# The inverse multiplied into b and r_b once for all chunks, in the RWKV part of a two-layer decoder trunk

## The chip, the cores and the metric

One core of one Trainium2 chip runs the whole program. The metric is the device time of that core in microseconds (us). A hardware profile of one execution gives the span and what each engine did when: TensorE (PE, with its weight loads PEld), VectorE (DVE), ScalarE (ACT), GpSimd (POOL) and SyncE (SP), which issues most transfers.

## The reference

Two decoder layers over 256 tokens of width 1024. Each layer projects x, runs a sparse multi-query attention and an RWKV-7 time mix side by side, gates and adds their outputs, projects, normalizes, and ends with a convolutional GLU. The change is inside the time mix, whose core is a recurrence over tokens, for 16 heads of 64:

```python
def step(state, inp):
    r_t, w_t, k_t, v_t, kk_t, b_t = inp
    sa = jnp.einsum('bhvk,bhk->bhv', state, -kk_t)
    state = state * w_t[:, :, None, :] + sa[..., None] * b_t[:, :, None, :] + v_t[..., None] * k_t[:, :, None, :]
    return state, jnp.einsum('bhvk,bhk->bhv', state, r_t)
```

The kernel computes it in chunks of 64 tokens: within a chunk the sequential dependence is a triangular system, whose inverse is built once per chunk, and the state is carried from chunk to chunk.

## The kernel before

**Rounds and units.** A round is 4 heads (GROUPS = 4 rounds a layer, 8 in all; r = 4*layer + g). It has GB = 2 blocks of 128 partitions (two heads each, 64 partitions a head) and NCH = 4 chunks, so NU = 8 units of 128 x 64. `wkv` (L976) writes out what TensorE does in a round, with semaphores between it and the other engines; ScalarE's and VectorE's parts are in their own loops (L1635 and L2342).

**A round.** Gram matmuls (L992) need, from the round before, `y_sum` on VectorE and `rkV` on ScalarE. Then LEVELS = 6 levels build the inverse: TensorE computes W = nT*X and XW = Y*W, ScalarE copies W out, VectorE updates X under a mask and transposes it into Y. The last level (L1062) computes `WtY` by `joined`, two 32 x 32 matmuls a unit, and VectorE updates Y with it; X isn't completed. Then come the steps over the chunks c = 0 to 3 (L1095 to L1130): 

- Z: the carried state S is multiplied with a and r (`Z{c}`, not for c = 0); VectorE adds akV (`chunk_z`, L1920).
- Q: Y times Z, together with rk times V for this chunk; ScalarE copies Q from PSUM to `Qs` (`chunk`, L1491).
- S and y: bt times Qs gives the state's update, rb times Qs the chunk's output; VectorE makes the new state (`chunk_s`, L1930).

At the end VectorE adds the outputs (`y_sum`, L1943), then centers them.

**Dense pieces.** TensorE's waits in a round are filled with pieces of the projections x*W (rkv of the next round, gates, and so on). A piece is 2 of 8 blocks of a product for one weight slot: six 128x256 matmuls, since each float32 product is made of three rounded ones (`product`, L768: hi*hi, hi*lo, lo*hi). Four pieces use up one weight slot. A round has 32 pieces and so eight slots. The tables LEVEL_GAPS and CHUNK_GAPS say in which gap each piece goes; `fill(n)` issues those of gap n. The chunk steps hold 20 pieces (19 in the last round of a layer), in gaps 14 to 24.

**Mids.** Before TensorE can use a slot, ScalarE casts it into `mid_hi` (L1342) and VectorE subtracts that from the slot (L1758). There are two `mid_hi` buffers, so the cast for slot m waits until TensorE has used slot m-2. `mids_up_to(mids_by(gap))`, at fixed places in both engines' code, makes those whose buffer is free by that gap; the places decide what stands behind what in these queues. Refills of the weight ring (four slots) are issued by SP as slots are used.

**Preparation of the next round** (not in the last round of a layer) is mixed into the steps: on TensorE `prep_1`, `prep_v`, `prep_rnT`, `prep_rnx` (L869); on ScalarE two tanh (L1413) and `prep_exp` (L1416: three exponentials and one more map); on VectorE decay and scan, `prep_keys`, `prep_keys_scaled`, `prep_arc`, `prep_bk`, and `prep_v` (three operations, layer 1 only).

**Helpers seen in the rows.** L930 is `per_head`, L936 `crossed`, L961 `swapped`: each issues one matmul per head, 64 x 64, for a unit. A float32 matmul of that kind has two records. In a chunk block a `per_head` and a `swapped` or `crossed` go side by side.

Of the kernel before, what the change touches and what calls it, by code (L numbers as in the profile page):

```python
# [66 lines left out]
CH = 64  # L67
# [18 lines left out]
CHUNK_GAPS = ([[14, 14, 14, 15, 17, 17, 18, 18, 19, 19, 20, 20, 21, 21, 22, 22, 23, 23, 24, 24]] * (GROUPS - 1)  # L86
              + [[14, 14, 15, 16, 16, 17, 17, 18, 19, 19, 20, 20, 21, 22, 22, 23, 23, 24, 24]])
# [3 lines left out]
GAPS = 14 + 3 * NCH  # L91
# [121 lines left out]
def trunk(nc, x_in, pos_in, stream, lora_in, cpar_in, rpar_in, const_in, masks_in, out, x_dram, v_dram):  # L213
    ctx = ExitStack()
    with ctx:
# [292 lines left out]
        def norm_steps(l, w):  # L508
            if l == DEPTH - 1 and w == "B":
# [42 lines left out]
                                    [f"XW{l}{k}" if l < LEVELS - 1 else f"WtY{l}{k}" for k in range(2)]) for l in lv], [])  # L552
                          + sum([[f"Z{c}"] * (c > 0) + [f"Q{c}"] + ([f"S{c}"] if c < NCH - 1 else []) + [f"y{c}"]
                                 for c in range(NCH)], []))
# [6 lines left out]
                           + [f"Q{c}" for c in range(NCH - 1)] + ["rkV_first", f"Q{NCH - 1}", "rkV"])  # L561
        act_y = by_round("act_y", ["sq", "yn"])
        dve_wkv = by_round("dve_wkv", ["Y0", "X0", "nTrb", "akrk"]
                           + sum([([f"X{l}{k}"] if l < LEVELS - 1 else []) + [f"Y{l}{k}"] for l in lv for k in range(2)], [])
# [153 lines left out]
        def _(pe):  # L718
# [257 lines left out]
            def wkv(r, fill):  # L976
# [58 lines left out]
                for lev in range(2, LEVELS):  # L1035
                    for k in range(2):
# [4 lines left out]
                        for u in range(4 * k, 4 * k + 4):  # L1041
                            dst = half64("W", k)[:, u - 4 * k, :]
                            if lev < BLOCKED:
                                w = per_head(dst, nT, X[:, u, :], u)
                            elif lev < LEVELS - 1:
                                w = per_block(dst, nT, X, u)
                            else:
                                w = across(dst, nT, X, u, 0, block_cols(1), block_cols(0))
                            if u == 4 * k + 3:
                                w.then_inc(*pe_wkv.inc(r, f"W{lev}{k}"))  # L1050
                            if lev == LEVELS - 1 and k == 1:
                                wty = joined(u - 4)
                            if lev == 2 and u < len(step_units):
                                if u == 0:
                                    pe.wait_ge(*act_wkv(r, "tokK"))
                                v = step_units[u]
                                side = swapped(unit64(5)[:, u, :], kt[:, v, :], Vc[:, v, :])
                                if u == len(step_units) - 1:
                                    side.then_inc(*pe_wkv.inc(r, "ktV"))
                        if k == 0:  # L1060
                            fill(2 + 2 * lev)
                    if lev == LEVELS - 1:  # L1062
                        wty.then_inc(*pe_wkv.inc(r, f"WtY{lev}0"))
# [3 lines left out]
                        for u in range(4, NU):  # L1067
                            wty = joined(u)
                        wty.then_inc(*pe_wkv.inc(r, f"WtY{lev}1"))
# [23 lines left out]

                pe.wait_ge(*act_wkv(r, "ktV"))
                for c in range(NCH):  # L1095
                    if c:
                        pe.wait_ge(*dve_wkv(r, f"S{c - 1}"))
                    s_old = S[:, (c + 1) % 2, :, :]
                    y = [unit64(5)[:, u, :] for u in bc(c)]
                    if c:  # L1100
                        for b, u in enumerate(bc(c)):
# [4 lines left out]
                    fill(14 + 3 * c, c == 0)  # L1106
                    pe.wait_ge(*dve_wkv(r, f"Z{c}" if c else f"Y{LEVELS - 1}1"))
                    if c == 0 and g + 1 < GROUPS:
                        pe.wait_ge(*act_prep(r + 1, "thw"))
                    if c == NCH - 1:  # L1110
                        pe.wait_ge(*act_wkv(r, "rkV_first"))
# [8 lines left out]
                    pe.wait_ge(*act_wkv(r, f"Q{c}"))  # L1120
                    for b, u in enumerate(bc(c)):
                        if c < NCH - 1:
                            mm = per_head(step64(2)[:, b, :], bt, Qs[:, b, :], u)
                            if b == GB - 1:
                                mm.then_inc(*pe_wkv.inc(r, f"S{c}"))
                        mm = crossed(y[b], rb, Qs[:, b, :], u, start=(c == 0), stop=(c == 0 or b == GB - 1))
# [3 lines left out]
                    fill(16 + 3 * c)  # L1130
# [194 lines left out]
        def _(act):  # L1325
# [165 lines left out]
            def chunk(r, c):  # L1491
                act.wait_ge(*pe_wkv(r, f"Q{c}"))
                act.copy(Qs[:, :, :], step64(3)).then_inc(*act_wkv.inc(r, f"Q{c}"))

            def rkv_out(r, c):

                steps = {NCH - 2: range(NCH - 1), NCH - 1: [NCH - 1]}.get(c, [])
                if len(steps):
                    n, a = len(steps), steps[0] * GB * CH
                    src = ps[:, 7, a:a + n * GB * CH].rearrange("p (c b s) -> p c b s", b=GB, s=CH)  # L1500
                    dst = yt[:, :, :].rearrange("p (b c) s -> p c b s", b=GB)[:, steps[0]:steps[0] + n]
                    for q, o in zip(HEADS, OTHER):
                        last = act.copy(dst[o], src[q])
                    last.then_inc(*act_wkv.inc(r, "rkV" if c == NCH - 1 else "rkV_first"))

            for l in L2:
# [128 lines left out]
                for g in range(GROUPS):  # L1635
# [41 lines left out]
                    for c in range(NCH):  # L1677
                        mids_up_to(l, mids_by(GAPS * g + 13 + 3 * c))
# [64 lines left out]
        def _(dve):  # L1743
# [158 lines left out]
            def level(r, lev):  # L1902
                for k in range(2):
                    if lev < LEVELS - 1:
                        dve.wait_ge(*pe_wkv(r, f"XW{lev}{k}"))
                        update(r, X, f"X{lev}{k}", 1, lev, k)
# [8 lines left out]
                    else:  # L1915
                        dve.wait_ge(*pe_wkv(r, f"WtY{lev}{k}"))
                        update(r, Y, f"Y{lev}{k}", 0, lev, k)
# [237 lines left out]
            for l in L2:  # L2155
# [186 lines left out]
                for g in range(GROUPS):  # L2342
# [25 lines left out]
                    for c in range(NCH):  # L2368
                        if c:
# [3 lines left out]
                            mids_up_to(l, mids_by(GAPS * g + 13 + 3 * c))  # L2373
# [20 lines left out]
                        if c in (1, 2):  # L2394
                            mids_up_to(l, mids_by(GAPS * g + 15 + 3 * c))
# [161 lines left out]
```

## Time and profile before

| | us |
|---|---|
| median of 3 runs | 1107.33 (1106.68 to 1109.58) |
| the profiled execution | 1107.22 |
| its span | 1105.4 |
| PE busy | 1077.7 (97%) |
| DVE busy | 802.7 (73%) |
| ACT busy | 569.6 (52%) |

Times in the rows below are us from the start of the span. A row of a timeline has start, duration, engine, line, operation, output and inputs, shapes and count; what stands in brackets is the engine's idle time before it and what ended that. Matmuls overlap one another, so from one matmul to the next the starts count, not the durations.

### The profile page before, as it was taken

To read this page: it belongs to the slowest core of one execution; us is meant where nothing else is said; L and a number is where in the kernel's file an instruction comes from. 1 tells how busy PE (TensorE), PEld (TensorE's weight loads), DVE (VectorE), ACT (ScalarE), POOL (GpSimd) and SP (SyncE) were. 2 spreads that over 40 slices of the span, in tenths; PEclk is the share of its full clock that TensorE was granted. 3 is DMA by queue.
4 is the path that set the end of the run, shared out by engine and by line. 5 is a ranking of instruction groups with operands and counts; after the bars stand their busy time and mean duration, and the time that the engine had idled before them with its cause. 6 is when DMAs were issued, how large, how long until landed. Compare 5 with 4: busy or idle time off the path is not lost. (4 is left out here: it accounts for less than half of the span.)

```text
span 1105.4 us, 31915 instructions
## 1 busy us (share of the span) xinstructions
PE 1077.7 (97%) x13568; PEld 977.2 (88%) x13568; DVE 802.7 (73%) x1471; ACT 569.6 (52%) x1008; POOL 72.2 (7%) x61
## 2 busy tenths in 40 slices
PE   8999999999999999999999999999999999999996
PEld 8878888888997999998898888888888979999885
DVE  3678787868676877774557887878876778777645
ACT  3653555555544555553246445555565445555531
POOL 0000010101001000000100000202011010000001
PEclk9999999999999999999999999999999999999998
DMA  8533232322564666566474323222326637566661
GB/s 302 166 102 118 72 101 80 95 90 89 191 229 135 211 190 189 186 200 197 134 236 142 121 88 98 89 86 81 98 64 229 210 128 226 189 185 189 210 188 56
DMA packets 45526, 165.58 MB, mean 150 GB/s; under 512 B 5168, under 2 KB 5424, under 8 KB 45136
## 3 DMA queue, kind: packets, MB, share of 16 engines
q1 hardware_dynamic: 42736, 154.03, 43.4%
q0 software_dynamic: 1504, 7.47, 2.2%
q8 instruction: 108, 1.77, 0.7%
q10 hardware_dynamic: 1152, 2.10, 0.6%
q14 instruction: 26, 0.21, 0.1%
HBM read 160.44 MB, written 3.15 MB: 148 GB/s over the span
## 5 line engine op out<-in xcount | busy, mean ns | idle before, releaser
L771 PE MATMUL ps<-x_tok_r,mid_hi 128*128 128x256 f32 x576 | 177.1, 307 | 0.5 <-DVE ring_r L1758 0.5
L773 PE MATMUL ps<-x_tok_r,ring_r 128*128 128x256 f32 x576 | 162.2, 282 | 0.0
L772 PE MATMUL ps<-yb_hi,mid_hi 128*128 128x256 f32 x576 | 162.1, 281 | 0.0
L1758 DVE TENSOR_TENSOR ring_r<-ring,mid_hi 128x1024 fp32r<-128x1024 f32 x80 | 97.2, 1216 | 31.1 <-ACT mid_hi L1342 31.0
L771 PEld LDWEIGHTS ps<-x_tok_r,mid_hi 128*128 128x128 f32 x576 | 108.5, 188 | 9.5 <-issue 1.4
L772 PEld LDWEIGHTS ps<-yb_hi,mid_hi 128*128 128x128 f32 x576 | 108.9, 189 | 0.7 <-issue 0.7
L773 PEld LDWEIGHTS ps<-x_tok_r,ring_r 128*128 128x128 f32 x576 | 108.9, 189 | 0.0
L1342 ACT CAST mid_hi<-ring 128x1024 fp32r<-128x1024 f32 x80 | 83.8, 1048 | 34.3 <-PE ps L773 26.6
L2021 DVE TENSOR_TENSOR rs_ks_r<-ring,tha_kkn_r 128x1024 fp32r<-128x1024 f32 x44 | 53.9, 1224 | 19.9 <-ACT tha_kkn_r L1394 19.7
L2021 DVE TENSOR_TENSOR vs_dC_r<-ring,b_k_r 128x1024 fp32r<-128x1024 f32 x44 | 53.7, 1220 | 17.6 <-ACT b_k_r L1394 17.6
L2021 DVE TENSOR_TENSOR X_Y_r<-ring,arc_r 128x1024 fp32r<-128x1024 f32 x42 | 51.3, 1222 | 19.8 <-ACT arc_r L1394 19.8
L2021 DVE TENSOR_TENSOR w_lo<-ring,w_hi 128x1024 fp32r<-128x1024 f32 x42 | 51.4, 1224 | 18.0 <-ACT w_hi L1394 17.9
L1394 ACT CAST tha_kkn_r<-ring 128x1024 fp32r<-128x1024 f32 x44 | 45.9, 1044 | 32.9 <-PE ps L773 32.9
L1394 ACT CAST arc_r<-ring 128x1024 fp32r<-128x1024 f32 x42 | 43.8, 1043 | 28.8 <-PE ps L773 19.6
L1394 ACT CAST b_k_r<-ring 128x1024 fp32r<-128x1024 f32 x44 | 45.9, 1043 | 20.1 <-PE ps L773 20.1
L772 PE MATMUL ps<-oT_r,tha_kkn_r 128*128 128x256 f32 x192 | 54.0, 281 | 0.0
L772 PE MATMUL ps<-oT_r,b_k_r 128*128 128x256 f32 x192 | 53.6, 279 | 0.0
L772 PE MATMUL ps<-oT_r,arc_r 128*128 128x256 f32 x192 | 53.6, 279 | 0.0
L772 PE MATMUL ps<-oT_r,w_hi 128*128 128x256 f32 x192 | 53.5, 279 | 0.0
L1394 ACT CAST w_hi<-ring 128x1024 fp32r<-128x1024 f32 x42 | 43.8, 1044 | 15.5 <-PE ps L773 15.2
L771 PE MATMUL ps<-xT_r,tha_kkn_r 128*128 128x256 f32 x176 | 49.9, 283 | 0.6 <-DVE oT_r L2103 0.6
L773 PE MATMUL ps<-xT_r,rs_ks_r 128*128 128x256 f32 x176 | 49.4, 281 | 0.0
(487 smaller groups left out, 3326.0 us busy)
## 6 DMA issues: line engine op xcount, KB each, us to landing
ring<-stream_dram SPq DMA_DIRECT2D x281, 512.0 KB, 3.7
lora_w<-lora_dram POOLq DMA_DIRECT2D x2, 1536.0 KB, 7.2
W_bt<-rpar_dram POOLq DMA_DIRECT2D x4, 512.0 KB, 5.1
kt_V<-rpar_dram POOLq DMA_DIRECT2D x4, 512.0 KB, 7.1
x_tok<-x_dram SPq DMA_DIRECT2D x2, 512.0 KB, 4.7
v_saved_dram<-vs_dC ACTq DMA_DIRECT2D x4, 256.0 KB, 4.5
x_tok<-x_dram SPq DMA_DIRECT2D x1, 1024.0 KB, 6.2
vf<-v_saved_dram ACTq DMA_DIRECT2D x4, 256.0 KB, 3.8
```

The costliest lines, as they stand in the source:

```text
L771: pe.matmul(dst, lh, rh, start=start, stop=False)
L772: pe.matmul(dst, lh, rl, start=False, stop=False)
L773: return pe.matmul(dst, ll, rh, start=False, stop=stop)
L1342: act.copy(mid_hi[m % NM][:, :], ring[:, n % RING, :]).then_inc(*act_mid.inc(l, m))
L1394: act.copy(w_hi[m % NS], ring[:, n % RING, :]).then_inc(*act_split.inc(l, m))
L1758: dve.tensor_tensor(rounded["ring"][:, k, :], ring[:, k, :], f32(mid_hi[m % NM][:, :]), ALU.subtract).then_inc(*dve_mid.inc(l, m))
L2021: dve.tensor_tensor(w_lo[m % NS], ring[:, n % RING, :], f32(w_hi[m % NS]), ALU.subtract).then_inc(*dve_split.inc(l, m))
```

## The change

Q is gone. Since Q = Y*Z is only used as bt*Q and rb*Q, the inverse is multiplied into bt and rb instead, for all chunks at once and ahead of the steps (`byX` on TensorE, `by_x` on ScalarE). A step then has two blocks, Z and S with y, and uses Z (or akV) where it used Qs. For this X is what must be complete, so the last level updates the left half of X instead of the right half of Y. All rk*V products move into the `byX` block, and ScalarE copies them out at once in step 1. GAPS is 23 instead of 26, the same pieces lie in gaps 14 to 21, and the calls of `mids_up_to` and `pairs_done` get new gap numbers; some of them are no longer limited to steps 1 and 2.

```diff
-CHUNK_GAPS = ([[14, 14, 14, 15, 17, 17, 18, 18, 19, 19, 20, 20, 21, 21, 22, 22, 23, 23, 24, 24]] * (GROUPS - 1)
-              + [[14, 14, 15, 16, 16, 17, 17, 18, 19, 19, 20, 20, 21, 22, 22, 23, 23, 24, 24]])
+CHUNK_GAPS = ([[14, 14, 14, 15, 15, 16, 16, 17, 17, 18, 18, 18, 19, 19, 19, 20, 20, 20, 21, 21]] * (GROUPS - 1)
+              + [[14, 14, 15, 15, 16, 16, 16, 17, 17, 18, 18, 18, 19, 19, 19, 20, 20, 21, 21]])
-GAPS = 14 + 3 * NCH
+GAPS = 15 + 2 * NCH
-    return [p for p, n in ends if n >= 14 and (n - 14) // 3 == c]
+    return [p for p, n in ends if n >= 14 and max(n - 15, 0) // 2 == c]
...
             def joined(u):
 
-                return across(half64("XW", u // 4)[:, u % 4, :], W, Y, u, 1, block_cols(0), block_cols(1))
+                for h in range(2):
+                    q = block_rows(h, 1)
+                    mm = pe.matmul(half64("XW", u // 4)[q, u % 4, 0:HB], Y[q, u, block_cols(1)], W[q, u, block_cols(0)],
+                                   start=True, stop=True)
+                return mm
...
+                fill(14, 1)
+                pe.wait_ge(*dve_wkv(r, f"X{LEVELS - 1}1"))
                 pe.wait_ge(*act_wkv(r, "ktV"))
+                if g + 1 < GROUPS:
+                    pe.wait_ge(*act_prep(r + 1, "thw"))
+                early = sum([bc(c) for c in range(NCH // 2)], [])
+                late = sum([bc(c) for c in range(NCH // 2, NCH)], [])
+                for i in range(len(early) + NU):
+                    if i < len(step_units):
+                        u = step_units[i]
+                        per_head(unit64(3)[:, u, :], X, bt[:, u, :], u)
+                    elif i < len(step_units) + len(late):
+                        u = late[i - len(step_units)]
+                        per_head(unit64(5)[:, u, :], X, rb[:, u, :], u)
+                    if i < len(early):
+                        u = early[i]
+                        mm = crossed(unit64(2)[:, u, :], X, rb[:, u, :], u)
+                    else:
+                        u = i - len(early)
+                        mm = swapped(rkv64(u % NCH)[:, u // NCH, :], rk[:, u, :], Vc[:, u, :])
+                mm.then_inc(*pe_wkv.inc(r, "byX"))
                 for c in range(NCH):
...
-                    fill(14 + 3 * c, c == 0)
-                    pe.wait_ge(*dve_wkv(r, f"Z{c}" if c else f"Y{LEVELS - 1}1"))
...
-                    for b, u in enumerate(bc(c)):
-                        swapped(rkv64(c)[:, b, :], rk[:, u, :], Vc[:, u, :])
-                        mm = per_head(step64(3)[:, b, :], Y, Zs[:, b, :] if c else akV[:, u, :], u)
-                    mm.then_inc(*pe_wkv.inc(r, f"Q{c}"))
-                    fill(15 + 3 * c)
+                    fill(15 + 2 * c)
...
-                    pe.wait_ge(*act_wkv(r, f"Q{c}"))
+                    pe.wait_ge(*(dve_wkv(r, f"Z{c}") if c else act_wkv(r, "rbX")))
                     for b, u in enumerate(bc(c)):
+                        z = Zs[:, b, :] if c else akV[:, u, :]
                         if c < NCH - 1:
-                            mm = per_head(step64(2)[:, b, :], bt, Qs[:, b, :], u)
+                            mm = per_head(step64(2)[:, b, :], bt, z, u)
...
-                    fill(16 + 3 * c)
+                    fill(16 + 2 * c)
...
+            def by_x(r):
+
+                act.wait_ge(*pe_wkv(r, "byX"))
+                dst, src = [t.rearrange("p (b c) s -> p b c s", b=GB)[:, :, 0:NCH - 1] for t in (bt, unit64(3))]
+                act.copy(dst, src).then_inc(*act_wkv.inc(r, "btX"))
+                dst, crossed, own = [t.rearrange("p (b c) s -> p b c s", b=GB) for t in (rb, unit64(2), unit64(5))]
+                for q, o in zip(HEADS, OTHER):
+                    act.copy(dst[q, :, 0:NCH // 2], crossed[o, :, 0:NCH // 2])
+                act.copy(dst[:, :, NCH // 2:], own[:, :, NCH // 2:]).then_inc(*act_wkv.inc(r, "rbX"))
...
                     for c in range(NCH):
-                        mids_up_to(l, mids_by(GAPS * g + 13 + 3 * c))
+                        mids_up_to(l, mids_by(GAPS * g + (14 + 2 * c if c else 13)))
...
-                        chunk(r, c)
+                        if c == 0:
+                            by_x(r)
                         if c == 0 and nxt:
                             prep_exp(r + 1)
-                        if c in (1, 2):
-                            mids_up_to(l, mids_by(GAPS * g + 15 + 3 * c))
-                        rkv_out(r, c)
+                        mids_up_to(l, mids_by(GAPS * g + 15 + 2 * c))
+                        if c == 1:
+                            rkv_out(r)
...
                 if lev == LEVELS - 1:
-                    out, mask, src = out[:, :, HB:CH], mask[:, :, HB:CH], src[:, :, 0:HB]
+                    out, mask, src = out[:, :, 0:HB], mask[:, :, 0:HB], src[:, :, 0:HB]
...
-                            mids_up_to(l, mids_by(GAPS * g + 13 + 3 * c))
+                            mids_up_to(l, mids_by(GAPS * g + 14 + 2 * c))
...
-                        if c in (1, 2):
-                            mids_up_to(l, mids_by(GAPS * g + 15 + 3 * c))
+                        mids_up_to(l, mids_by(GAPS * g + 15 + 2 * c))
                         if nxt and c == 0:
                             prep_pend(r + 1)
```

## Rows read from the trace of the kernel before

**Rows 1.** The page: span, and busy time of the engines

```profile
span 1105.4 us, 31915 instructions
...
PE 1077.7 (97%) x13568; PEld 977.2 (88%) x13568; DVE 802.7 (73%) x1471; ACT 569.6 (52%) x1008; POOL 72.2 (7%) x61
```

**Rows 2.** Who waited for whom, TensorE: total, times, longest

```profile
PE ps L869 <- DVE ang L1803: 0.7, 3, 0.2
```

**Rows 3.** Stretches: length, then busy time (and instructions) of each engine

```profile
668.38:693.48 25.10, 24.84 (x330) 21.96 (x324) 19.33 (x39) 14.91 (x32) 1.64 (x1) 1.00 0.30 92
...
173.14:198.02 24.88, 24.54 (x326) 21.69 (x322) 17.91 (x38) 14.41 (x30) 1.65 (x1) 1.00 0.31 90
```

**Rows 4.** Timeline of TensorE, 670 to 675 us, a round of layer 1

```profile
670.19 0.39 PE L771 MATMUL ps<-x_tok_r,mid_hi 128*128 128x256 f32 x1
...
671.81 0.27 PE L961 MATMUL ps<-kt_V,ak_rk 64*64 64x64 f32 x2
...
671.82 0.27 PE L930 MATMUL ps<-sq,X_Y 64*64 64x64 f32 x2
...
671.91 0.23 PE L961 MATMUL ps<-kt_V,ak_rk 64*64 64x64 f32 x2
...
672.04 0.23 PE L930 MATMUL ps<-sq,X_Y 64*64 64x64 f32 x2
...
672.20 0.39 PE L771 MATMUL ps<-x_tok_r,mid_hi 128*128 128x256 f32 x1
...
673.46 0.27 PE L930 MATMUL ps<-Qs,W_bt 64*64 64x64 f32 x2
...
673.90 1.15 PE L869 MATMUL ps<-ang,const 8*128 8x128 f32 x8
...
674.98 0.27 PE L930 MATMUL ps<-S,arc 64*64 64x64 f32 x2
```

**Rows 5.** The same, step 2, and the end of the round

```profile
683.22 0.27 PE L961 MATMUL ps<-kt_V,ak_rk 64*64 64x64 f32 x2
...
691.87 0.28 PE L772 MATMUL ps<-yb_hi,mid_hi 128*128 128x256 f32 x1
...
693.05 0.28 PE L773 MATMUL ps<-x_tok_r,ring_r 128*128 128x256 f32 x1
...
693.48 0.33 PE L930 MATMUL ps<-arc,b_k 64*64 64x128 f32 x2
```

**Rows 6.** Timeline of ScalarE in the same round

```profile
672.34 0.27 ACT L1493 COPY Qs<-ps 128x128 f32<-128x128 f32 x1 [0.47 <-PE ps L930]
...
673.68 0.63 ACT L1420 ACTIVATE dA<-dB 128x512 f32<-128x512 f32 x1 [1.08 <-DVE vs_dC L1790]
...
676.25 1.03 ACT L1342 CAST mid_hi<-ring 128x1024 fp32r<-128x1024 f32 x1
...
684.99 0.96 ACT L1503 COPY yt<-ps 64x384 f32<-64x384 f32 x2
```

**Rows 7.** Timeline of VectorE in the same round

```profile
677.31 1.23 DVE L1758 TENSOR_TENSOR ring_r<-ring,mid_hi 128x1024 fp32r<-128x1024 f32 x1 [1.34 <-ACT mid_hi L1342]
...
678.45 0.87 DVE L1749 SCALAR_TENSOR_TENSOR rs_ks<-ps,cpar,rs_ks 128x255 f32<-128x255 f32 x2
...
680.01 0.29 DVE L1938 TENSOR_TENSOR Sa<-ps,Sa 128x128 f32<-128x128 f32 x1
...
680.54 0.68 DVE L1840 TENSOR_TENSOR rs_ks<-rs_ks,tmp 128x512 f32<-128x512 f32 x1
...
682.88 0.28 DVE L1923 TENSOR_TENSOR Zs<-ps,sq 128x128 f32<-128x128 f32 x1
...
685.80 0.29 DVE L1938 TENSOR_TENSOR Sa<-ps,Sa 128x128 f32<-128x128 f32 x1
...
690.59 0.69 DVE L1814 TENSOR_TENSOR scratch<-vf,vs_dC 128x512 f32<-128x512 f32 x1
...
692.65 0.68 DVE L1947 TENSOR_TENSOR yt<-ps,yt 128x512 f32<-128x512 f32 x1
```

More of the change, by code:

```diff
@@ L551, in trunk @@
                                  + (["XW10", "XW11", "akV"] if l == 1 else
-                                    [f"XW{l}{k}" if l < LEVELS - 1 else f"WtY{l}{k}" for k in range(2)]) for l in lv], [])
-                          + sum([[f"Z{c}"] * (c > 0) + [f"Q{c}"] + ([f"S{c}"] if c < NCH - 1 else []) + [f"y{c}"]
-                                 for c in range(NCH)], []))
+                                    [f"XW{l}{k}" for k in range(2)]) for l in lv], [])
+                          + ["byX"] + sum([[f"Z{c}"] * (c > 0) + [f"S{c}"] * (c < NCH - 1) + [f"y{c}"] for c in range(NCH)], []))
         pe_bonus = Steps(sem("pe_bonus"), [["zg", "bonus"] if r % GROUPS else ["bonus", "zg"] for r in range(R)])
@@ L560, in trunk @@
                                                                            for l in lv], [])
-                           + [f"Q{c}" for c in range(NCH - 1)] + ["rkV_first", f"Q{NCH - 1}", "rkV"])
+                           + ["btX", "rbX", "rkV"])
         act_y = by_round("act_y", ["sq", "yn"])
         dve_wkv = by_round("dve_wkv", ["Y0", "X0", "nTrb", "akrk"]
-                           + sum([([f"X{l}{k}"] if l < LEVELS - 1 else []) + [f"Y{l}{k}"] for l in lv for k in range(2)], [])
+                           + sum([[f"X{l}{k}"] + [f"Y{l}{k}"] * (l < LEVELS - 1) for l in lv for k in range(2)], [])
                            + sum([[f"Z{c}", f"T{c}"][0:2 if c < NCH - 1 else 1] * (c > 0) + [f"S{c}a", f"S{c}"] * (c < NCH - 1)
@@ L1067, in wkv @@
                         for u in range(4, NU):
-                            wty = joined(u)
-                        wty.then_inc(*pe_wkv.inc(r, f"WtY{lev}1"))
+                            xw = joined(u)
+                        xw.then_inc(*pe_wkv.inc(r, f"XW{lev}1"))
                         continue
@@ L1119, in wkv @@
                         prep_rnT(r + 1)
-                    pe.wait_ge(*act_wkv(r, f"Q{c}"))
+                    pe.wait_ge(*(dve_wkv(r, f"Z{c}") if c else act_wkv(r, "rbX")))
                     for b, u in enumerate(bc(c)):
+                        z = Zs[:, b, :] if c else akV[:, u, :]
                         if c < NCH - 1:
-                            mm = per_head(step64(2)[:, b, :], bt, Qs[:, b, :], u)
+                            mm = per_head(step64(2)[:, b, :], bt, z, u)
                             if b == GB - 1:
                                 mm.then_inc(*pe_wkv.inc(r, f"S{c}"))
-                        mm = crossed(y[b], rb, Qs[:, b, :], u, start=(c == 0), stop=(c == 0 or b == GB - 1))
+                        mm = crossed(y[b], rb, z, u, start=(c == 0), stop=(c == 0 or b == GB - 1))
                     mm.then_inc(*pe_wkv.inc(r, f"y{c}"))
@@ L1489, in levels, with rkv_out @@
                     act.copy(ktV[:, :, :], unit64(5)[:, 0:(NCH - 1) * GB, :]).then_inc(*act_wkv.inc(r, "ktV"))
[L1491 to L1504, printed above, removed]
+            def by_x(r):
[6 more added lines that the diff above has]
+                act.copy(dst[:, :, NCH // 2:], own[:, :, NCH // 2:]).then_inc(*act_wkv.inc(r, "rbX"))
+            def rkv_out(r):
+                src = ps[:, 7, :].rearrange("p (c b s) -> p c b s", b=GB, s=CH)
+                dst = yt[:, :, :].rearrange("p (b c) s -> p c b s", b=GB)
+                for q, o in zip(HEADS, OTHER):
+                    last = act.copy(dst[o], src[q])
+                last.then_inc(*act_wkv.inc(r, "rkV"))
             for l in L2:
@@ L1903, in level @@
                 for k in range(2):
+                    dve.wait_ge(*pe_wkv(r, f"XW{lev}{k}"))
+                    update(r, X, f"X{lev}{k}", 1, lev, k)
                     if lev < LEVELS - 1:
[L1905 to L1906 removed]
                         dve.wait_ge(*dve_wkv(r, f"X{lev}{k}"))
```

16 lines of the change are left out of this document (4 added, 12 removed).

## The prediction

> **What bounds the kernel now.** The page first: TensorE shows work for 1077.7 of 1105.4 us [rows 1]. The list of who waited for whom then says how little of TensorE's time around this change is waiting: of the waits that touch these steps the largest listed one is 0.7 us in three pieces [rows 2]. So the kernel is bound by what TensorE has to issue, and a change can win only by giving it less, and loses as soon as it makes it wait. The busy time by stretches gives the size of the stage: from the first dense piece of gap 14 to the first Gram matmul of the next round it is 25.10 us in a round of layer 1 and 24.88 us in one of layer 0, with VectorE busy for 19.33 and 17.91 of it [rows 3]. In layer 1 VectorE has under 6 us of slack in the stage, and takes its work strictly in the order of the code.
>
> Then the timelines of one such round, engine by engine. On TensorE a chunk step is a block of four 64-row slots: it begins 1.62 us after the first matmul of two dense pieces, and the next dense matmul begins 0.39 later; one block with its two pieces takes 2.01 us [rows 4]. A dense piece alone costs 6 matmuls at 0.118 (691.87 to 693.05, ten from start to start) [rows 5], 0.70 us: so the block costs 2.01 - 1.41 = 0.60, of which the slots are 4 x 0.06 (671.91 to 672.04, two slots) and the rest, 0.36, is going into the small form and back out.
>
> **TensorE's own work.** Before, the four Q blocks of a round cost 4 x 0.60 = 2.40 us (the rk*Vc matmuls ride in the same slots). They become one block of 12 iterations, each of two slots: 0.60 + 20 x 0.06 = 1.80. That is 0.60 us less in each of 8 rounds, 4.8 in all, although there are 12 more products. The last level still has two matmuls per unit, with other rows and columns; the old and the new pair differ in the column block that they share with the W matmuls. No row has that pairing in 32-row form, so I bound it by nothing and by one slot of 0.06 for each of 8 units, 0.5 us a round; I take nothing, because in 64-row form L961 and L930 share column halves and start 0.01 apart [rows 4].
>
> At that same place the Trainium skill, "TensorEngine Tiling (Array Packing)", section "Restrictions and Gotchas", says that different row tiles can't access one PSUM bank at the same time. Taken for both heads of a product, that would double the 24 slots, 1.44 us a round. The row with L961 x2 and L930 x2 (each pair is two heads, one bank) shows them starting together, so the trace speaks against it here.
>
> Waits that the new order removes, if nothing else goes wrong: Q of step 2 starts at 683.22 where the rhythm (674.98 + 4 x 2.01) gives 683.02, 0.2 late, right behind Zs on VectorE [rows 4, 5, 7]; there are six such rounds, 1.2 us. The matmuls of L869 (eight rows) wait 0.7 us in three rounds [rows 2]. The Gram matmuls of layer 1 start 0.43 after the last dense matmul instead of 0.21, three times 0.2 [rows 5]. Together 2.5 at most.
>
> **The new order, walked through** in a round of layer 1 with the rows' durations. byX starts at 671.81 as Q0 did, its last slot at 671.81 + 0.10 + 22 x 0.06 = 673.23, and the next dense matmul at 673.39. ScalarE begins 0.30 after a last slot [rows 4, 6]. Its copies into b and r_b have 384 columns and three times 256. The nearest row is 64x384 twice in 0.96 [rows 6]; from that and the 0.27 for 128 columns I take 0.42 + 3 x 0.32 = 1.4 us (at least four of the 0.27, 1.1; at most four of 0.48, 1.9). They end at 674.93. TensorE meanwhile does two pieces and the two small prep products, and wants r_b at 675.35: this wait costs nothing. It would cost once the copies take more than 1.8.
>
> But behind them on ScalarE stand prep_exp, 673.68 to 676.25, 2.57 us, which used to run beside Q0 and step 0, and then the cast of the fifth dense slot (rows say 1.03) [rows 6]. They end at 677.50 and 678.53. On VectorE the subtraction of that slot now stands ahead of pend and Z1 (before: behind Z1), so VectorE waits for ScalarE until 678.56 and is done at 679.79. TensorE by then: step 0 at 675.35, L869 at 675.79, dense at 676.87 (it took 1.08), Z1 at 678.49, dense at 678.89, and the fifth slot's first piece at 679.70. It waits 0.15.
>
> VectorE then has, without a gap: pend, Z1 and T 0.5 (three of its smallest operations, 0.1 to 0.2 each), the shift-add and the keys 1.56, the S pair 0.53, the scaled keys and the sixth slot 2.34 + 0.09 [rows 7]: ready at 684.8. TensorE has in the same time the rest of gap 17, step 1, the three pieces of gap 18 and Z2, and wants the sixth slot, now the first piece of gap 19 (it was in gap 21), at 683.77. **First real stall: 1.1 us.** Next, step 2 of VectorE gets the third shift-add in front of arc and b, k: Z2, T, arc, b and k 2.92, a slot 1.14, the shift-add 0.78, the S pair 0.53: counted from 684.7, where Z2 begins, S2 is ready at 690.1, and TensorE asks at 689.89: 0.2 us.
>
> The end of the round is worse. A new call at the end of step 3 puts the subtraction for the next round's second slot ahead of y_sum. VectorE: Z3 690.73, a slot to 692.08, v (layer 1 only, 690.59 to 692.65, 2.06) to 694.14, the new slot 1.14 to 695.28, y_sum 0.68 to 695.96. The Gram matmuls wait for y_sum. TensorE arrives at 694.24, since only two pieces and not four stand between Z3 and y3. **Stall 1.8 us**, Gram at 696.0 where it was at 693.48 [rows 5]: +2.5 a round. In layer 0 v is absent, but the new slot's cast can start only when TensorE has used the last slot (about 692.1), so cast 1.05, subtraction 1.23 and y_sum 0.65 end at 695.0; the round is 26.6 long against 24.88, +1.75 [rows 3].
>
> The last round of each layer has no prep: VectorE has gaps there, and the saved 0.60 stays. And since y_sum is now the releaser, the centering and the masks that follow it come later relative to the Gram matmuls: y_sum began 0.83 ahead of them [rows 5, 7], now 0.72; in layer 0, without v, it must have been further ahead, for which I have no row. Between 0.1 and 0.5, I put 0.2 on each of six rounds. The shift of a subtraction out of the next round saves TensorE nothing, as that one stood behind the masks and had no reader waiting. Loads on SP's queue keep their order and count; POOL is not touched.
>
> Sum: 3 x 2.5 + 3 x 1.75 - 2 x 0.6 + 6 x 0.2 = +12.75 us. The profiled execution took 1107.22 us, 0.11 under the median of the three runs, so the sum goes on it unchanged: **1120.0 us**.
>
> **Rivals.** (1) Faster: TensorE's own work decides. 4.8 + 2.5 less is 1099.9 us. For it: TensorE is busy throughout, and the saving in blocks is plain. It needs VectorE to have the sixth slot by 683.77, one microsecond earlier than walked, and y_sum by 694.2; that is so only if copies and prep_exp together hold ScalarE under about 2.9 us where I count 4.0. Against it: prep_exp alone is 2.57. Chance 0.15.
> (2) Only the end of the round waits: the middle stalls dissolve as VectorE catches up, and 1.0 us (layer 0) to 1.3 (layer 1) are left: -7.3 + 3 x 1.0 + 3 x 1.3 = -0.4, 1106.8 us. For it: VectorE has 1.34 us idle ahead of the fifth slot in the old trace [rows 7]. Against it: that very idle time is what the later cast takes. Chance 0.12.
> (3) More than forecast: the 32-row matmuls at their upper bound, 8 x 0.5, and the copies at 1.9, which moves the whole chain behind them, 6 x 0.5: 7 more, 1127 us. Chance 0.07.
> (4) The two heads of a product exclude each other in a bank and byX takes 48 slots: 8 x 1.44 = 11.5 more, less what the stalls hide, some 1125 us. Against it: the pairs that start together [rows 4]. Chance 0.01. The Trainium skill has this rule, in "TensorEngine Tiling (Array Packing)", "Restrictions and Gotchas".
>
> The forecast has 0.65.
>
> **Numbers.** 0.3% (3.3 us) is about what a measurement of this kernel can tell from no change. Faster has rival 1 and a little of 2, 0.16; the same has most of 2, 0.11; slower 0.73. The forecast's own range is 1114 to 1125 us, from stalls 1 us smaller in each of six rounds to copies and late masks at their upper bounds. The range given takes in rival 2 and rival 3, 1104 to 1127; rival 1 lies outside.
>
> **What would show it.** Right: byX as one run of about 1.45 us; six waits of TensorE for the sixth slot's subtraction (L1758's successor) of about 1 us; Gram matmuls released by y_sum, 1 us late in layer 0 and near 2 in layer 1; the stage at 26.6 us in layer 0 and 27.6 in layer 1; the last rounds shorter by 0.6. Wrong: the same stretches at or under 24.9 with VectorE's subtraction ahead of TensorE, or a wait of TensorE for r_b, which I hold at nothing.

## The result, and the profile after

The changed kernel takes 1121.28 us (median of 6 runs, 1119.04 to 1123.88) against 1107.01 us for the kernel before on the same chip: ratio 1.0128, interval 1.0105 to 1.0152, 1.3% slower. The profiled execution took 1122.55 us with a span of 1120.7 us, 15.3 more than before.

The head of the page, kernel after:

```profile
span 1120.7 us, 32270 instructions
...
PE 1079.5 (96%) x13760; PEld 981.3 (88%) x13760; DVE 801.7 (72%) x1471; ACT 573.5 (51%) x992; POOL 72.4 (6%) x61
```

TensorE's busy time is 1.8 us longer than in [rows 1], so of the 15.3 us almost all (13.5) is TensorE standing still. For whom, the list of waits says (kernel after, TensorE: total, times, longest):

```profile
PE ps L929 <- DVE yt L1961: 8.8, 6, 1.8
PE ps L770 <- DVE ring_r L1775: 6.8, 10, 0.9
```

The first line was not there before, and of the second kind there was one wait of 0.5 us. L929 is the Gram matmul of the next round, which waits for y_sum; L770 is a dense piece that waits for its subtraction. Both are VectorE's.

The busy time by stretches, kernel after: a stage of layer 1, one of layer 0, and the one of layer 0's last round (up to the first matmul of o_hi with tha_kkn_r); columns as in [rows 3]:

```profile
677.00:704.56 27.56, 24.74 (x353) 22.09 (x348) 20.18 (x40) 15.89 (x30) 1.64 (x1) 1.00 0.31 100
121.45:148.39 26.94, 24.50 (x351) 21.84 (x346) 18.28 (x37) 15.16 (x28) 1.64 (x1) 1.00 0.29 94
285.36:304.85 19.49, 19.36 (x311) 17.69 (x307) 11.97 (x21) 10.75 (x16) 0.00 (x0) 1.00 0.49 164
```

Against [rows 3] that is +2.46 us in layer 1 and +2.06 in layer 0, and the three rounds of each layer agree within 0.01. The last rounds went from 19.89 to 19.49, -0.40. Over all eight stages (3 x 2.46 + 3 x 2.07 - 0.78): +12.8 of the 15.3 us. The levels between the stages add 1.35, the rest of the kernel 1.1.

TensorE's timeline, kernel after, round of layer 1: the byX block with the dense matmuls around it, the sixth slot, the Gram.

```profile
680.21 0.28 PE L772 MATMUL ps<-x_tok_r,ring_r 128*128 128x256 f32 x1
680.42 0.27 PE L929 MATMUL ps<-W_bt,X_Y 64*64 64x64 f32 x2
680.43 0.27 PE L935 MATMUL ps<-nT_rb,X_Y 64*64 64x64 f32 x2
680.53 0.23 PE L929 MATMUL ps<-W_bt,X_Y 64*64 64x64 f32 x2
...
681.98 0.39 PE L770 MATMUL ps<-x_tok_r,mid_hi 128*128 128x256 f32 x1
...
693.54 0.36 PE L770 MATMUL ps<-x_tok_r,mid_hi 128*128 128x256 f32 x1 [0.92 <-DVE ring_r L1775]
...
704.56 0.33 PE L929 MATMUL ps<-arc,b_k 64*64 64x128 f32 x2 [1.77 <-DVE yt L1961]
```

byX takes 1.56 us from its first matmul to the next dense one. The last line answers to 693.48 in [rows 5]: then the Gram waited 0.2 us at most, starting 0.43 after the last dense matmul where the pitch is 0.21.

ScalarE, kernel after, same round: the three kinds of by_x copies, prep_exp's first line, and the cast of the fifth slot.

```profile
682.10 0.48 ACT L1508 COPY W_bt<-ps 128x384 f32<-128x384 f32 x1 [1.62 <-PE ps L964]
682.61 0.75 ACT L1511 COPY nT_rb<-ps 64x256 f32<-64x256 f32 x2
683.37 0.38 ACT L1512 COPY nT_rb<-ps 128x256 f32<-128x256 f32 x1
683.63 0.63 ACT L1433 ACTIVATE dA<-dB 128x512 f32<-128x512 f32 x1
...
686.19 1.04 ACT L1355 CAST mid_hi<-ring 128x1024 fp32r<-128x1024 f32 x1
```

VectorE, kernel after, same round: the subtractions for slots five and six, and the end of the stage:

```profile
687.26 1.23 DVE L1775 TENSOR_TENSOR ring_r<-ring,mid_hi 128x1024 fp32r<-128x1024 f32 x1 [2.13 <-ACT mid_hi L1355]
...
692.18 1.22 DVE L1775 TENSOR_TENSOR ring_r<-ring,mid_hi 128x1024 fp32r<-128x1024 f32 x1
...
701.99 0.69 DVE L1837 SCALAR_TENSOR_TENSOR vs_dC<-scratch,vs_dC 128x512 f32<-128x512 f32 x1
702.59 1.22 DVE L1775 TENSOR_TENSOR ring_r<-ring,mid_hi 128x1024 fp32r<-128x1024 f32 x1
703.73 0.68 DVE L1961 TENSOR_TENSOR yt<-ps,yt 128x512 f32<-128x512 f32 x1
```

Read it from below: y_sum ends at 704.41 and the Gram starts 0.15 later; ahead of y_sum stands a subtraction that no one needs before the next round's levels. From 687.26 on VectorE is idle once for 0.55 us (ahead of Z3). The one large gap is the 2.13 us in front of the fifth slot, for ScalarE's cast behind prep_exp.

Layer 0 ends otherwise. ScalarE and VectorE there, kernel after, ahead of the Gram at 148.39:

```profile
145.34 1.05 ACT L1355 CAST mid_hi<-ring 128x1024 fp32r<-128x1024 f32 x1 [2.52 <-PE ps L772]
...
146.42 1.23 DVE L1775 TENSOR_TENSOR ring_r<-ring,mid_hi 128x1024 fp32r<-128x1024 f32 x1 [1.34 <-ACT mid_hi L1355]
147.56 0.68 DVE L1961 TENSOR_TENSOR yt<-ps,yt 128x512 f32<-128x512 f32 x1
```

VectorE has no v here and is idle for 1.34 us: it waits for the cast, and the cast for TensorE's last matmul on the buffer. So in layer 1 the stage ends by VectorE's own queue, in layer 0 by the hand-over from TensorE to ScalarE to VectorE.

### The profile page after: what moved, and what is told of

It is laid out like the page before. It is cut to its first block, busy times and chain, and to the rows that moved or that the text cites. A ratio compares the mean times of both kernels' runs of the same rounds, so it can differ in the third digit from the quotient of the medians.

```text
span 1120.7 us, 32270 instructions
## 1 busy us (share of the span) xinstructions
PE 1079.5 (96%) x13760; PEld 981.3 (88%) x13760; DVE 801.7 (72%) x1471; ACT 573.5 (51%) x992; POOL 72.4 (6%) x61
## 4 chain that ended last, share of the span: by engine, by line
PE 78%; DVE 14%; ACT 4%; issue 3%; DMA 1%; POOL 1%; DVEq 0%; SPq 0%; ACTq 0%
PE ps L770 19%; PE ps L771 18%; PE ps L772 17%; PE ps L929 5%; PE ps L1156 3%; DVE ring_r L1775 3%; PE ps L745 2%; PE ps L943 2%; PE ps L970 1%; PE ps L1214 1%; PE ps L1230 1%; ACT mid_hi L1355 1%; PE ps L964 1%; DMA ring<-stream_dram 1%; PE ps L884 1%
## 5 line engine op out<-in xcount | busy, mean ns | idle before, releaser
L770 PE MATMUL ps<-x_tok_r,mid_hi 128*128 128x256 f32 x576 | 176.4, 306 | 7.1 <-DVE ring_r L1775 6.8
L770 PEld LDWEIGHTS ps<-x_tok_r,mid_hi 128*128 128x128 f32 x576 | 108.6, 189 | 17.1 <-issue 7.5
L1900 DVE COPY_PREDICATED X_Y<-masks,ps 128x256 f32<-128x256 uint32 (+1 forms) x80 | 33.0, 415 | 29.8 <-PE ps L929 17.8
L770 PE MATMUL ps<-xT_r,tha_kkn_r 128*128 128x256 f32 x176 | 49.4, 281 | 0.6 <-DVE oT_r L2117 0.6
```

The costliest lines, as they stand in the source:

```text
L770: pe.matmul(dst, lh, rh, start=start, stop=False)
L1900: dve.copy_predicated(out, mask, src).then_inc(*dve_wkv.inc(r, name))
```

## The experiments

The theory: the stage is now set by one serial chain, ScalarE's cast of the fifth slot, then VectorE's queue up to S of step 2, and from there to y_sum by one of the two ends above, so that work on that chain costs up to its own length. The rival: TensorE's work, or the products over all chunks, is the cost itself. All but e8 start from the changed kernel. Stage lengths are read like those above, for one round of each kind; the other rounds of the kind agree within 0.03 us, but for one round each of e2, e4, e6, e10 and e11, which is 0.06 to 0.17 longer (in e10 and e11 a stretch at half the clock reaches into it). The ratio is to the kernel before as run beside each experiment (medians 1106.32 to 1107.01 us), so it is the better of the two to compare. There is no e9.

| run | time, us | ratio to before | stage, layer 0 | layer 1 | last round |
|---|---|---|---|---|---|
| before | 1107.01 | 1 | 24.87 | 25.10 | 19.89 |
| after | 1121.28 | 1.0128 (1.0105 to 1.0152) | 26.94 | 27.56 | 19.49 |
| e1 | 1117.46 | 1.0096 (1.0078 to 1.0114) | 25.70 | 26.41 | 19.48 |
| e2 | 1116.85 | 1.0097 (1.0076 to 1.0119) | 26.08 | 26.91 | 19.49 |
| e3 | 1119.48 | 1.0131 (1.0099 to 1.0163) | 26.92 | 27.55 | 19.48 |
| e4 | 1112.56 | 1.0052 (1.0037 to 1.0067) | 24.88 | 25.80 | 19.48 |
| e5 | 1110.21 | 1.0031 (1.0008 to 1.0053) | 24.87 | 25.79 | 19.48 |
| e6 | 1105.07 | 0.9982 (0.9966 to 0.9998) | 24.07 | 25.27 | 19.49 |
| e7 | 1109.43 | 1.0027 (1.0016 to 1.0039) | 24.09 | 24.30 | 19.49 |
| e8 | 1116.96 | 1.0080 (1.0057 to 1.0103) | 26.11 | 26.23 | 19.88 |
| e10 | 1104.80 | 0.9976 (0.9962 to 0.9990) | 24.09 | 24.28 | 19.48 |
| e11 | 1123.45 (one run) | | 27.43 | 28.05 | 19.98 |

**e1: y_sum ahead of the last subtraction** (VectorE alone)

```
                        if nxt and c == 1:
                            prep_keys_scaled(r + 1)
-                       mids_up_to(l, mids_by(GAPS * g + 15 + 2 * c))
+                       if c < NCH - 1 or not nxt:
+                           mids_up_to(l, mids_by(GAPS * g + 15 + 2 * c))
...
                    y_sum(r)
                    if nxt:
+                       mids_up_to(l, mids_by(GAPS * g + 15 + 2 * (NCH - 1)))
                        prep_bonus(r + 1)
```

> The changed kernel, and on VectorE alone the last subtraction of step 3 (the one that belongs to the next round's second gap) is issued behind y_sum instead of ahead of it, in the six rounds that have a next round. Theory (that subtraction waits for its cast and so delays y_sum, for which the gram waits): TensorE's idle time before the gram falls from 1.15 us to under 0.3 in layer 0 and from 1.8 to under 0.8 in layer 1, three times each; the time falls by 4 to 7 us, to 1114 to 1117 us. Rival (the added time is TensorE's own work, the last-level products over all chunks are no cheaper in the end): the idle time before the gram may fall, but what follows it starts no earlier, and the time stays within 1 us of 1121.

TensorE's waits in e1:

```profile
PE ps L929 <- DVE yt L1961: 1.9, 3, 0.6
PE ps L970 <- DVE ak_rk L1886: 3.6, 6, 0.8
```

The Gram's wait fell from 8.8 to 1.9 us and the stage by 1.24 and 1.15 us. In layer 1 that is about the subtraction (1.23) gone from VectorE's queue. In layer 0 the likeness to 1.23 is chance: there cast and subtraction together left the path, and what TensorE got back is the 1.21 us that it had waited in front of the Gram. But the subtraction now stands ahead of the masked products, and half of the gain comes back as a wait for ak_rk in the first level. The time fell by 3.8 us, just short of the 4 to 7 expected.

**e2: the fifth cast ahead of prep_exp** (ScalarE alone)

```
                        if c == 0 and nxt:
+                           mids_up_to(l, mids_by(GAPS * g + 15))
                            prep_exp(r + 1)
```

> The changed kernel, and ScalarE casts the fifth slot's piece between the copies of byX and the exponentials of the next round, instead of behind them. Theory (the fifth subtraction stands ahead of pend and Z1 on VectorE and idles there 2.1 us): that subtraction starts about 2.6 us earlier, the idle time before the sixth slot's dense piece (0.9 us) falls to 0.3 or less unless the exponentials, now 1 us later, delay the keys; time 1 to 5 us under 1121. Rival (the exponentials set the pace: pend and the keys wait for them): the subtraction is earlier but pend and all behind it are 1 us later, gram later; time 1121 to 1127.

The stages fell by 0.86 and 0.65 us, the time by 4.4: inside the 1 to 5 expected, near the upper end. The fifth subtraction came 2.2 us earlier, where 2.6 was expected; only a part of that is gained, since VectorE then waits 1.24 us for Z1. TensorE's longest wait for a subtraction fell from 0.9 to 0.6 us and not to 0.3.

**e3: the sixth subtraction ahead of the scaled keys** (VectorE alone)

```
                        if nxt and c == 1:
+                           mids_up_to(l, mids_by(GAPS * g + 15 + 2 * c))
                            prep_keys_scaled(r + 1)
```

> The changed kernel, and VectorE does the subtraction for the sixth slot ahead of the scaled keys instead of behind them. Theory (the sixth slot's dense product waits for a subtraction that is queued behind 1.2 us of work it does not need): the 0.9 us of idle time before it go, six times; but y_sum at the end waits for casts as before, so that part of it comes back at S2 or the gram: time 1116 to 1121. Rival (TensorE's order is set by something else): no change, within 1 us of 1121.

```profile
PE ps L929 <- DVE yt L1961: 8.8, 6, 1.8
PE ps L929 <- DVE S L1954: 6.0, 6, 1.0
```

The waits of e3 show what a stall in the middle was worth: nothing. The sixth slot's wait went, a new one of 1.0 us for S came in each of six rounds, and the stages are the same within 0.02 us. Exchanging two operations on the chain leaves its end where it was, as the theory says for the Gram. The whole time says less: the median is 1119.48 us, but the ratio, 1.0131, is that of the changed kernel.

**e4: the three together**

> The three orders together. Theory (TensorE has 0.6 us less work in each round than in the kernel before, and what the change costs is only order on VectorE and ScalarE): the stage from the first step over chunks to the gram falls from 26.9 and 27.6 us to 25 us or less, the time to 1104 to 1110, level with the kernel before or a little under. Rival (the work over all chunks has a cost of its own on the path, such as the wait for by_x's copies): the stage stays above 26 us and the time above 1113.

The stages fell by 2.06 and 1.76 us; e1 and e2 alone give 2.10 and 1.80. That they add up speaks for one chain. But the time of 1104 to 1110 was missed, 1112.56, and so were the 25 us or less in layer 1: 25.80. TensorE's waits show the rest:

```profile
PE ps L929 <- DVE S L1955: 4.3, 6, 0.7
...
PE ps L970 <- DVE ak_rk L1887: 3.6, 6, 0.8
PE ps L929 <- DVE yt L1962: 1.9, 3, 0.6
```

These 9.8 us are the next three edits.

**e5: as e4, the last subtraction left to the levels** (the second hunk of e1 taken out: `grams` issues it behind the masked products, as in the kernel before)

> The three orders as in the fourth run (fifth cast ahead of the exponentials, sixth subtraction ahead of the scaled keys, no subtraction ahead of y_sum), but the last subtraction of step 3 is left to where the kernel before has it: behind the gram's four masked products, not right behind y_sum. Theory (behind y_sum it only moved the wait: the fourth run waited 0.6 us in each round for ak_rk in the first level): those six waits, 3.6 us in all, go; time 1107.5 to 1110. Rival (PE then waits for that piece in its second slot of the levels, or the masked products are set by the gram itself): the 3.6 us stay under another name, 1112 to 1113.

The waits for ak_rk are gone from the list and the stages unchanged; 1110.21 us, 2.4 less than e4 and at the upper end of the 1107.5 to 1110 expected.

**e6: as e5, S of step 2 ahead of arc and b_k** (VectorE)

```
                            elif nxt and c == 2:
+                               chunk_s(r, c)
                                prep_arc(r + 1)
                                prep_bk(r + 1)
...
-                       if c < NCH - 1:
+                       if c < NCH - 1 and not (nxt and c == 2):
                            chunk_s(r, c)
```

> As the run before this one, and in step 2 VectorE makes the state of the step (Sa and S) ahead of the next round's arc and b_k (four products, 2.8 us) instead of behind them. Theory (VectorE's queue sets the end of the stage): the 0.7 us that TensorE waits for S in each of six rounds go; in layer 0 all of it is kept, in layer 1 about 0.55 us, since y_sum is next there and waits 0.6 already; 3.5 to 4 us less than the run before, 1104 to 1106. Rival (arc and b_k, now 0.6 us later, hold y_sum or the gram up by as much): no gain, 1107 to 1110.

The stages fell by 0.80 and 0.52 us, 4.0 in six rounds, and the time by 5.1. Two stretches of e6, layer 0 and layer 1:

```profile
120.90:144.97 24.07, 24.06 (x351) 21.75 (x346) 17.88 (x38) 14.69 (x28) 1.64 (x1) 1.00 0.30 92
666.61:691.88 25.27, 24.35 (x352) 22.02 (x348) 19.23 (x39) 15.88 (x30) 1.64 (x1) 1.00 0.32 103
```

In layer 0 TensorE is busy for all of the stage: 24.07 is its own work, 0.80 under the kernel before. In layer 1 0.9 us of waiting for y_sum is left, behind v. Run again, in more rounds:

> The kernel of the run with S early, once more in more rounds. Theory (its stages are 0.80 us shorter than the kernel before in layer 0, 0.17 us longer in layer 1 and 0.40 us shorter in the last rounds, 2.7 us in sum; levels alike): the ratio to the kernel before is 0.9975, its interval wholly under 1. Rival (the 1.4 us seen are chance, from the short stretches at half the clock that each run has in another number): the interval reaches over 1.

1105.95 us, 0.9986 (0.9973 to 1.0000): level with the kernel before or a hair faster. The interval ends at 1, so the two cases are not told apart.

**e7: as e6, v behind y_sum, the bonus and the centring behind the next masked products** (VectorE)

```
-                           elif nxt:
-                               prep_v(r + 1)
...
                    y_sum(r)
                    if nxt:
-                       prep_bonus(r + 1)
-                       y_center(r)
+                       prep_v(r + 1)
...
                    grams(r)
-                   if g == 0:
-                       prep_bonus(r)
+                   prep_bonus(r)
+                   if g:
+                       y_center(r - 1)
```

> As the run before this one, and VectorE does the next round's v (three products in layer 1) behind y_sum, and the bonus and the centring of y behind the masked products of the next gram. Theory: the gram's wait for y_sum in layer 1 (0.6 to 0.8 us, three times) goes, TensorE has its own work alone on the path and the stage is 24.3 us in both layers, 0.6 under the kernel before: 1101 to 1104. Rival (v or the centred y is then late for the levels): waits of 0.3 to 1 us a round come in the first two levels, 1104 to 1109.

The stage of layer 1 is 24.30, as the theory has it. The time is 1109.43 us, the rival's and a little over:

```profile
PE ps L970 <- DVE yt L1979: 6.5, 7, 1.1
```

The centred y is turned on TensorE in the first levels, and was late there.

**e10: as e7, the centring back behind v, ahead of the Gram's products; only the bonus behind the masked products**

> As the run with S early, with the next round's v behind y_sum, but now the centring of y stays ahead of the gram's products and only the bonus goes behind them. Theory: the centred y is no longer late (the 1.1 us a round that L970 waited in the run with v late go), and in layer 1 the gram's wait of 0.9 us goes three times; v adds 2 us ahead of the masked products there, of which 0.3 us or less shows: stage 24.3 us in layer 1, time 1102 to 1104. Rival (VectorE has no room between y_sum and the masked products, whatever stands there is waited for): L970 waits 0.7 to 1.1 us for ak_rk in layer 1, time 1104 to 1107.

Layer 1 in e10, its stretch, and its wait in the levels:

```profile
668.71:692.99 24.28, 24.28 (x353) 21.99 (x347) 17.90 (x37) 15.41 (x30) 1.64 (x1) 1.00 0.30 92
```

```profile
PE ps L970 <- DVE ak_rk L1887: 1.3, 3, 0.4
```

1104.80 us, 0.9976 (0.9962 to 0.9990). The time is over the 1102 to 1104 expected and in the rival's range; the wait for ak_rk, 0.4 us a round in layer 1, lies between the theory's 0.3 or less and the rival's 0.7 to 1.1, so VectorE had less room there than I thought, but some. This is the one version here whose interval lies clearly under the kernel before: by 0.24%, at the edge of what a measurement of this kernel can tell. Its computation is the changed kernel's, in another order.

**e8: the kernel before, with the early call alone**

```
-                       if c in (1, 2):
+                       if c in (1, 2) or c == 3 and nxt:
                            mids_up_to(l, mids_by(GAPS * g + 15 + 3 * c))
```

(the same line on ScalarE and on VectorE)

> The kernel before with one thing of the change: ScalarE casts and VectorE subtracts the last piece of step 3 inside step 3, ahead of y_sum. Theory (this call is what holds the gram up): the gram comes 1.2 to 1.8 us later in each of six rounds, idle before it 1.0 to 1.9 us, of which the levels give back up to 0.4 since ak_rk has one subtraction less ahead of it; time 5 to 10 us above the kernel before, 1112 to 1117. Rival (in the kernel before, y_sum has room of that size, and it is only the changed order of the pieces that uses it up): under 2 us above, 1106 to 1109.

1116.96 us, 1.0080: without any of the rest, the call costs 1.24 us a stage in layer 0 and 1.13 in layer 1. TensorE in e8, the Gram in each layer:

```profile
147.87 0.33 PE L930 MATMUL ps<-arc,b_k 64*64 64x128 f32 x2 [1.15 <-ACT X_Y L1641]
...
698.77 0.33 PE L930 MATMUL ps<-arc,b_k 64*64 64x128 f32 x2 [1.28 <-DVE yt L1947]
```

The first names ScalarE's reset of Y (147.18 to 147.80); y_sum ends at 147.72, so both come about together there. Both stand behind the cast of that piece, the one on ScalarE itself, the other through the subtraction.

**e11: the changed kernel, by_x's first copy made twice**

```
                act.copy(dst, src).then_inc(*act_wkv.inc(r, "btX"))
+               act.wait_ge(*act_wkv(r, "btX"))
+               act.copy(dst, src)
```

> The changed kernel, and ScalarE makes the first copy of by_x (bt, 0.48 us) twice. Theory (TensorE's first step product waits for the last of these copies where nothing else covers them): in the two last rounds the step product starts 0.48 us later or more, their stage 19.5 becomes 20.0 us; layer 0's first step product, which waits 0.08 us now, waits 0.5; in layer 1, where the products of the v path stand in between, 0.3 to 0.5; the stages grow by as much and by up to 0.5 more where the fifth cast is then later too: time 1123 to 1127. Rival (the copies are covered, and the last rounds' missing 0.2 us is TensorE's own work): last stages 19.5 as they are, under 1 us in all.

All stages grew by 0.48 to 0.50 us (one by 0.66, whose first 0.4 us lie in a stretch at half the clock), the last rounds from 19.49 to 19.98, and the wait shows. First the last round of layer 0 in the changed kernel, TensorE:

```profile
289.94 0.28 PE L772 MATMUL ps<-o_hi,ring_r 128*128 128x256 f32 x1
290.35 0.27 PE L929 MATMUL ps<-sq,W_bt 64*64 64x64 f32 x2
```

and the same step in e11:

```profile
290.68 0.27 PE L929 MATMUL ps<-sq,W_bt 64*64 64x64 f32 x2 [0.62 <-ACT nT_rb L1514]
```

In the changed kernel the step product starts 0.41 after the last dense matmul where 0.21 is the pitch (680.21 to 680.42 above), and the last copy ends at 290.29. So 0.2 us of waiting for r_b was there already, too short to be named; one more copy is paid in full.

## Why the prediction was right

It said 1120.0 us; the measurement is 1121.28. The mechanism is as forecast: TensorE has less to do, and waits for VectorE's subtractions and for y_sum cost more than that. Point by point:

- **TensorE saves 0.60 us a round in blocks.** Right: 1.56 us for byX with 1.58 forecast. The stages of e6 and e10 in which TensorE doesn't wait give the whole saving, 0.80 a round (24.87 to 24.07; in layer 1 25.10 to 24.28); in layer 0 that is the 0.60 and the 0.2 that Q of step 2 had waited (1.2 in six rounds).
- **The last level's 32-row pairs cost nothing.** Right as far as seen: the shortest levels of layer 1 are 26.37 us before and 26.38 after.
- **The heads share a bank without excluding each other.** The two heads of a product stand in one row of the timeline (x2), the products beside each other start 0.01 us apart, and the block takes 1.56 us; 24 slots more, at 0.06 each, would make it 3.0. The rule in the Trainium skill, "TensorEngine Tiling (Array Packing)", "Restrictions and Gotchas", that different row tiles can't access one PSUM bank at the same time, is not what this trace shows for heads that write different partitions.
- **Copies 1.4 us, no wait for r_b.** The copies took 1.53 on ScalarE's queue (682.10 to 683.63), a little over. **This is the step that failed:** "this wait costs nothing" holds where the next round's small products stand in between. In the last rounds, which have no such products, TensorE waited 0.2 us, and that is why they gained 0.40 and not 0.60. In the other rounds the room is small too: with the copies 0.48 longer, e11 lists eight waits, one in each round:

```profile
PE ps L929 <- ACT nT_rb L1514: 3.6, 8, 0.6
```

- **The fifth slot, ScalarE late.** Right in time: the subtraction was put 10.2 us after the stage's start and came at 10.26. What TensorE lost by it was taken too small, 0.15 us against 0.35 in layer 1 and 0.54 in layer 0 (by the starts of the dense matmuls around it).
- **The sixth slot, 1.1 us, and S2, 0.2.** Seen (0.92 listed, 1.0 over the pitch; 0.14 at S2). But e3 shows that such a stall is a symptom: removed alone, it came back at S of step 2, because VectorE's queue up to S was as long as before.
- **y_sum behind v and the early subtraction, Gram +2.5 us.** Right: y_sum was put 26.9 us after the stage's start and began at 26.73; stage 27.56 with 27.6 forecast. e1 and e8 show from both sides that the early call costs 1.1 to 1.2 us of it.
- **Layer 0 +1.75.** Measured +2.07. Cast, subtraction, y_sum and Gram took 3.05 us where I had 2.9, and the cast began 23.89 us into the stage and not 23.7.
- **Masks and centring 0.2 x 6.** Wrong: nothing of it came. VectorE's masking of the next round (L1892 before, L1909 after) starts 2.09 us behind the Gram in layer 1 in both kernels, since y_sum already released the Gram there before (it began 0.83 ahead of it, and does so now, where I took 0.72). In layer 0 y_sum was 1.43 ahead before and is 0.83 now, but the masking had to wait for TensorE there before:

```profile
148.23 0.74 DVE L1892 COPY_PREDICATED X_Y<-masks,ps 128x512 f32<-128x512 uint32 x1 [0.44 <-PE ps L997]
```

  That is 2.02 us behind the Gram at 146.21; after the change it is 150.48, 2.09 behind 148.39. The levels grew by 1.35 us in sum, but 1.7 of that is TensorE's clock in one round (below); without it they are 0.35 shorter.

So the sum came out well partly because errors cancel: the stages gave 12.8 us where the steps had 11.55 (1.0 more in layer 0, 0.4 more in the last rounds, 0.1 less in layer 1), and the 1.2 us of the levels did not come. The other 2.5 us of the span are the 1.35 in the levels and 1.1 outside these rounds, whose cause stays open.

The experiments also divide the loss. In layer 0 the gross loss, from the stage without waits to the changed kernel's, is 2.07 + 0.80 = 2.87 us a round: the early call 1.24 (e1), the fifth cast behind prep_exp 0.86 (e2), S behind arc and b_k 0.80 (e6), together 2.90. In layer 1 it is 2.46 + 0.82 = 3.28: 1.15, 0.65, 0.52 and, for v ahead of y_sum, 0.99 (e6 to e10), together 3.31. These are steps along one way, so they would nearly add up in any case; what closes the account is TensorE's timeline in the changed kernel. Measured against the usual distance from start to start, TensorE is late by 0.54 us at the fifth slot, 0.96 at the sixth, 0.14 at S of step 2 and 1.21 at the Gram in layer 0, 2.85 in sum, and by 0.35, 0.96, 0.13 and 1.84 in layer 1, 3.28. Nothing is left for the products over all chunks: they cost TensorE less, as forecast, and the loss in the stages is order alone. Rival 1's 1099.9 us was not reached by any order tried: with TensorE's stages all its own, but for the 0.2 us in the last rounds, e10 stands at 1104.80. Its stages are 5.4 us shorter in sum than before, but its levels are longer by some 1.2 without the first round, ak_rk's 1.3 us among it.

## What to carry to other kernels

When a change takes work from the engine that bounds the kernel, walk through the queue of the next busiest engine in code order before counting the gain: here a saving of 0.8 us a round became a loss of 2 to 2.5 because four pieces of work with later deadlines stood ahead of what TensorE waits for next. The early call was put there by the change, and with the new gap numbers the fifth subtraction moved ahead of Z1 and a shift-add ahead of S of step 2; prep_exp ahead of the cast, arc and b_k ahead of S, and v ahead of y_sum stood so before, and almost nothing waited for them until the steps became shorter and the copies came in front. (In layer 1 the Gram had waited 0.2 us behind v even then.) A stall in the middle of such a stage is not its cause; ask which operation ends the stage, list what stands ahead of it on its queue, and move from there what has no reader yet. Then look at what the moved piece now stands in front of: e3 only moved the wait, e1 moved half of it, and e7 more than it had gained.

## What the runs showed of the hardware

**TensorE's granted clock falls to half for 3.4 us at a time, and at two places of the program.** Leaving out the last microseconds, where TensorE has no more work, the 13 profiles of this case show 21 such stretches, one to three in each. Thirteen begin 63 to 65 us after the end of a layer's last round (eight in layer 0, five in layer 1). The other eight begin 3.0 to 3.8 us before the end of the levels of some round, another one each time. One of these fell into the changed kernel (stretches of the kernel after; the last three columns are granted clock, DMA share, GB/s):

```profile
170.00:173.60 3.60, 2.99 (x98) 2.69 (x97) 2.24 (x6) 2.83 (x6) 0.00 (x0) 1.00 0.50 150
173.60:177.00 3.40, 3.40 (x37) 3.13 (x28) 1.44 (x2) 0.71 (x3) 0.00 (x0) 0.50 0.02 5
```

The granted clock is 1.00 (2.4 GHz) up to 173.6, with TensorE busy for 2.99 of 3.60 us, and 0.50 (1.2 GHz) for 3.4 us, in which TensorE was busy throughout. Half of that time, 1.7 us, is the loss; the levels of this round took 28.63 us where the kernel before has 26.92. In e5 one made the levels of one round 29.24 us instead of the 27 around it.

At the first place the kernel before has one too, from 361.1 on:

```profile
360.00:370.00 10.00, 10.00 (x72) 9.74 (x73) 9.45 (x15) 3.74 (x10) 0.22 (x1) 0.83 0.38 114
```

TensorE was busy for only 1.91 of the 4 us ahead of it. But that work is the same in every profile, 1.91 to 1.93 us of four in both layers, and in 13 of these 26 cases the clock stayed at 1.00: the lighter stretch alone does not decide it. What does is open; nothing here tried it.

For reading a profile the lesson is to compare stage by stage, since one such stretch is as large as two thirds of what a round of layer 1 lost by the change. The stages of the table are of rounds at a clock of 1.00 and tell 0.1 us apart, while whole runs of one kernel scatter by 4 to 9 us in most of the sets here.
